# Context products of A, B and D as split products with the values stationary, with moved stages, in a hybrid five-branch decoder trunk

## What is computed

```python
pr = split_projection(x @ w_in)              # D_MODEL 1024 -> all branches' q, k, v, z, g
o_a = dsa_attention(aq, ak, av, iq, ik, pr['i_w'])   # causal, top 128 keys of an index score
o_b = moba_attention(bq, bk, bv)             # here: causal over both blocks of 256
o_c = rms_norm(diff_attention(cq, ck, cv, lam), diff_norm) * (1.0 - lam_init)
o_d = mla_attention(qn, qr, kn, kr, dv)      # causal, from low-rank latents
o_e = memory_attention(e_q, mk, mv)          # 256 memory tokens
# each: s = q k^T * scale; p = softmax(s); o = p v
y = o * jax.nn.silu(z)
u = jnp.einsum('btnc,ncd->btnd', y, w_branch)
out = jnp.sum(jax.nn.sigmoid(g) * u, axis=2) @ w_out
x = layer_norm(DN_ALPHA * x + out, ln_g, ln_b)
```

## Time and profile before

| | us |
|---|---|
| median of 3 runs | 1381.6 |
| range of the runs | 1380.46 to 1382.38 |
| profiled execution, its own time | 1384.15 |
| its span, first to last instruction | 1382.5 |

### The profile page before, as it was taken

The page is one execution under the profiler, slowest core; times in us unless marked ns, Lnnn a source line. Parts: engine busy times, 40 slices in busy tenths (PEclk is TensorE's granted clock), DMA queues, the critical chain, the costliest instruction groups (busy, mean ns, idle before and its releaser), DMA issues.

```text
span 1382.5 us, 19021 instructions
## 1 busy us (share of the span) xinstructions
PE 1328.0 (96%) x6872; PEld 1130.7 (82%) x6872; DVE 661.8 (48%) x1609; ACT 653.3 (47%) x1296; POOL 669.9 (48%) x850
## 2 busy tenths in 40 slices
PE   6999999999988999999999999999999899999995
PEld 5888878888877898888888888888888779888884
DVE  4646696433155753213265668753322665432044
ACT  4455345454275664423245543555434665643232
POOL 3543453255563444467464435334446434645764
PEclk9899999999998999999999999999999999999998
DMA  7322242231331143232413223223123213323221
GB/s 258 114 77 62 81 114 58 67 88 47 103 95 37 37 123 107 58 107 77 140 49 106 68 71 106 81 58 85 53 74 111 59 33 86 95 65 100 84 77 61
DMA packets 147052, 116.47 MB, mean 84 GB/s; under 512 B 5520, under 2 KB 131856, under 8 KB 146704
## 3 DMA queue, kind: packets, MB, share of 16 engines
q1 hardware_dynamic: 146816, 114.22, 27.8%
q10 hardware_dynamic: 144, 1.05, 0.2%
HBM read 112.10 MB, written 3.15 MB: 83 GB/s over the span
## 4 chain that ended last, share of the span: by engine, by line
PE 79%; DVE 12%; ACT 4%; issue 2%; POOL 1%; DMA 1%; SPq 0%; POOLq 0%; DVEq 0%; ACTq 0%
PE product L737 19%; PE product L738 18%; PE product L739 18%; PE context L977 5%; PE scores L949 3%; PE transposed L962 3%; PE branch_product L737 2%; PE branch_product L739 2%; PE branch_product L738 2%; DVE index_scores L1389 2%; DVE top_eight L1395 1%; DMA residual<-in_x_dram 1%; ACT score_operands L1001 1%; POOL residual L677 1%; DVE vector_scratch L1214 1%
## 5 line engine op out<-in xcount | busy, mean ns | idle before, releaser
L721 POOL TENSOR_TENSOR weights_rest<-raw_weights,weights_head 128x320 fp32r<-128x320 f32 (+3 forms) x672 | 540.1, 836 | 376.8 <-ACT weights_head L1001 376.8
L737 PE MATMUL product<-weights_head,stationary_head 128*128 128x512 f32 (+3 forms) x768 | 291.4, 379 | 7.8 <-POOL weights_rest L721 7.6
L1001 ACT ACTIVATE weights_head<-raw_weights 128x1280 fp32r<-128x1280 f32 (+4 forms) x178 | 198.3, 1115 | 200.3 <-PE product L739 153.5
L739 PE MATMUL product<-weights_head,stationary_rest 128*128 128x512 f32 (+3 forms) x768 | 285.6, 372 | 0.0
L738 PE MATMUL product<-weights_rest,stationary_head 128*128 128x512 f32 (+3 forms) x768 | 285.4, 372 | 0.0
L737 PE MATMUL product<-stationary_head,weights_head 128*128 128x512 f32 x640 | 263.5, 412 | 0.0
L738 PE MATMUL product<-stationary_rest,weights_head 128*128 128x512 f32 x640 | 252.6, 395 | 0.0
L739 PE MATMUL product<-stationary_head,weights_rest 128*128 128x512 f32 x640 | 252.1, 394 | 0.0
L704 POOL TENSOR_TENSOR merged<-merged,activated 128x256 f32<-128x256 f32 x128 | 93.0, 748 | 291.4 <-DVE activated L1533 291.2
L737 PEld LDWEIGHTS product<-weights_head,stationary_head 128*128 128x128 f32 x768 | 145.7, 190 | 29.8 <-POOL weights_rest L721 8.4
L739 PEld LDWEIGHTS product<-weights_head,stationary_rest 128*128 128x128 f32 x768 | 145.4, 189 | 23.7
(11 more groups left out here) (200 smaller groups left out, 1812.5 us busy)
## 6 DMA issues: line engine op xcount, KB each, us to landing
raw_weights<-in_w_in_dram SPq DMA_DIRECT2D x104, 512.0 KB, 3.7
raw_weights<-in_w_in_dram SPq DMA_DIRECT2D x72, 256.0 KB, 2.9
raw_weights<-in_w_branch_dram SPq DMA_DIRECT2D x80, 128.0 KB, 3.7
raw_weights<-in_w_out_dram SPq DMA_DIRECT2D x16, 512.0 KB, 3.6
merged<-in_w_mem_kv_dram SPq DMA_DIRECT2D x8, 512.0 KB, 7.3
raw_weights<-in_w_in_dram SPq DMA_DIRECT2D x8, 416.0 KB, 3.1
raw_weights<-in_w_in_dram SPq DMA_DIRECT2D x8, 296.0 KB, 3.8
residual<-in_x_dram SPq DMA_DIRECT2D x4, 512.0 KB, 11.4
```

The costliest lines, as they stand in the source:

```text
L721: ins = nc.gpsimd.tensor_tensor(WL[:, sw, part], RAW[:, sr, part], WH[:, sw, part].bitcast(F32), ALU.subtract)
L737: nc.tensor.matmul(dst, sh, mh, start=start, stop=False)
L739: return nc.tensor.matmul(dst, sl, mh, start=False, stop=stop)
L1001: return nc.scalar.activation(dst, src, ACT.Copy, scale=scale)
```

## The change

- **Contexts of A, B and D.** `wide_steps` takes the place of `att_steps` for them. The transposed probabilities of two tiles are kept side by side, ACT's copy as fp32r heads, and DVE makes their rests (`pr`, new tile of 1024 columns), after which alone TP is free. The values of a head are split as well (`vs` on ACT, `vr` on DVE): head and rest, 64 columns each, are one stationary operand of 128. A context product moves 256 (both tiles) or 128 (the diagonal block of the second) columns of heads or rests of the probabilities. There is one `V` for two tiles. Bank O then holds the context transposed, the part by the values' heads in one half of the rows and that by their rests in the other: ACT copies one (`fo`), DVE adds the other (`fa`).
- **Gates.** 1/row sum is multiplied into the gate (`fin`), the gate is transposed (`zj`, bank G2 or TP), and DVE multiplies it into the context; `yj` is then a copy and a subtraction from SBUF, without transposes.
- **Places** of B, A and C attention, top of tile 3, A out and lambda are moved.
- **C.** The operand copies and rests are cut into four parts a head; the join `W` and the transposes `T` lie further apart; its first transposes use banks U and O.
- **Order of groups** in IX and O1, of the first steps, and of the norms at a layer's end; the fourth tile of x is loaded after two weight units; `ahead` is gone.

```diff
+WIDE = "ABD"
+def wide_steps(b):
+    if b == "D":
+        out = [[("qt", b, 0)], [("ev", b, 0)], [("er", b, 0), ("qt", b, 1)], [("ev", b, 1)], [("er", b, 1)], [("vs", b, 0), ("vr", b, 0)]]
+    else:
+        out = [[("qt", b, 0)], [("ev", b, 0), ("er", b, 0)], [("ev", b, 1), ("er", b, 1)], [("vs", b, 0), ("vr", b, 0)]]
+    for i in range(UNITS + LAG_V + 1):
+        first, second = [], []
+        u = i - LAG_V
+        j = u // NT
+        if 0 <= u < UNITS and u % 2 == 1:
+            first.append(("V", b, u))
+        if 0 <= i - LAG_T < UNITS:
+            first.append(("T", b, i - LAG_T))
+            second.append(("pr", b, i - LAG_T))
+        if u >= NT and u % NT == 0:
+            first.append(("fa", b, j - 1))
+            if j < NH:
+                second.append(("vr", b, j))
+        if i < UNITS:
+            second.append(("S", b, i))
...
+        out += [first, second]
...
-    ("B attention", ("gE0", 1, 0), ("gE1", 3, 3), 0.0),
-    ("top of tile 3", ("gE0", 0, 1), ("gE1", 2, 3), 0.0),
+    ("B attention", ("gE0", 0, 1), ("gE1", 3, 3), 0.0),
+    ("top of tile 3", ("gE0", 2, 0), ("gE1", 3, 4), 0.0),
-    ("A attention", ("gB0", 0, 2), ("gB1", 3, 3), 0.0),
-    ("A out", ("gB1", 3, 4), ("C0", 0, 3), 0.0),
-    ("lambda", ("gB1", 3, 3), ("C0", 0, 2), 0.0),
-    ("C attention", ("gA0", 0, 0), ("D0", 3, 2), 0.0),
+    ("A attention", ("gB0", 0, 2), ("C0", 1, 2), 0.0),
+    ("A out", ("C0", 1, 3), ("C0", 2, 2), 0.0),
+    ("lambda", ("gB0", 2, 0), ("gB0", 2, 0), 0.0),
+    ("C attention", ("C1", 0, 2), ("D0", 3, 1), 0.0),
...
+            order = [(0, 0), (1, 0), (0, 1), (1, 1), (2, 0), (2, 1), (0, 2), (1, 2), (0, 3), (2, 2), (1, 3), (2, 3)] + [(3, t) for t in range(NT)]
+        elif c == "O1":
+            order = [(0, t) for t in range(NT)] + [(1, 0), (1, 1), (2, 0), (3, 0), (2, 1), (3, 1)] + [(u, t) for t in (2, 3) for u in range(1, 4)]
...
-    start = [("ln0", 0), ("ln0", 1), ("mkv", 0), ("ln0", 2), ("xj", 0, 0), ("xj", 0, 1), ("ln0", 3), splits[0], ("mkv", 1),
-             ("xj", 1, 0), ("xj", 1, 1), ("ln0", 4), splits[1], splits[2]]
+    start = [("ln0", 0), ("ln0", 1), ("mkv", 0), ("ln0", 2), ("xj", 0, 0), ("xj", 0, 1), splits[0], splits[1], ("ln0", 3), ("mkv", 1),
+             ("xj", 1, 0), ("xj", 1, 1), splits[2], ("ln0", 4)]
...
+                    elif kind == "V" and step[1] in WIDE:
+                        _, b, u = step
+                        j, t = divmod(u, NT)
+                        ph, pl, vs = wide(b)
+                        if t == 1:
+                            claim("O")
+                            pe.wait_ge(rest.sem, rest.at(L, ("vr", b, j)))
+                        pe.wait_ge(rest.sem, rest.at(L, ("pr", b, u)))
+                        blocks = [(0, ph), (t, ph), (t, pl)] + [(i, p) for i in range(1, t) for p in (ph, pl)]
+                        blocks.insert(3 if t == 1 else 1, (0, pl))
+                        for n, (i, p) in enumerate(blocks):
+                            at = P if i == t else 0
+                            last = nc.tensor.matmul(O[:, (t - 1) * P + at:(t + 1) * P], vs[:, i].rearrange("p c d -> p (c d)"),
+                                                    p[:, i, at:2 * P], start=n == 0, stop=n == len(blocks) - 1)
...
-                        freed["TP"] = (moved, L, step)
+                        freed["TP"] = (rest, L, ("pr", b, u)) if b in WIDE else (moved, L, step)
```

More of the change, by code:

```diff
@@ L131, in diff_steps @@
             first.append(("S", "C", 2 * i))
[L132 removed]
+            second.insert(0, ("S", "C", 2 * i + 1))
         if 0 <= i - 1 < UNITS:
[L134 to L146 removed]
+            first.append(("W", i - 1))
+        if i == 3:
+            second.append(("qt", "C", 1))
+        out += [first + early.get(2 * i, []), second + early.get(2 * i + 1, [])]
     return out
@@ L587, in _ @@
             load_mk(0, 2)
-            load_x(3)
             load_mk(0, 3)
@@ L858, in _ @@
                         freed[name] = (rest, L, ("x", t, j))
+                    elif kind == "yj" and step[1] in WIDE:
+                        continue
+                    elif kind == "zj":
+                        _, b, k = step
+                        name, bank = z_bank(k)
+                        claim(name)
+                        pe.wait_ge(final.sem, final.at(L, (b, 2 * k + 1)))
+                        for t in range(NT):
+                            last = nc.tensor.transpose(bank[:, t * P:(t + 1) * P],
+                                                       VZ[:, vz(b), t, BW + k * P:BW + (k + 1) * P], ident)
+                        last.then_inc(t_done.sem, t_done.step(step))
+                        freed[name] = (gated, L, step)
                     elif kind == "yj":
@@ L1119, in _ @@
                         act.wait_ge(t_done.sem, t_done.at(L, step))
-                        copy(PT[:, 0:w], TP[:, 0:w]).then_inc(moved.sem, moved.step(step))
+                        if b in WIDE:
+                            half = slice(t % 2 * P, (t % 2 + 1) * P)
+                            copy(wide(b)[0][:, 0:t + 1, half], TP[:, 0:w].rearrange("p (i n) -> p i n", n=P)).then_inc(moved.sem, moved.step(step))
+                        else:
+                            copy(PT[:, 0:w], TP[:, 0:w]).then_inc(moved.sem, moved.step(step))
                     elif kind == "lam":
```

233 lines of the change are left out of this document (158 added, 75 removed).

## The result

The changed kernel takes 1367.4 us (median of 4 runs, 1366.2 to 1369.6) against 1381.8 before (median of 4 runs; the 1381.6 above is that of three of them): a ratio of 0.9899, 95% interval 0.9882 to 0.9916. The forecast was 1350. The direction was right, and of 32 us of gain 14.4 came. The profiled execution has a span of 1368.0 against 1382.5.

What follows compares the result with a forecast made beforehand. TensorE was taken as the bound, busy 1328.0 of 1382.5 us. The terms -17 + 10 + 4 - 3 + 6 - 21 - 4.5 - 1.5 - 5 sum to -32, from the median 1381.6 to 1350 us; range 1330 to 1374.

Steps and rivals of the forecast that it cites:

- Contexts, -17: Context products of A, B and D: 1.40 us a head, 0.70 less, over 24 heads; -17 us.
- rival 4: Units of A, B and D: chained transposes, copy and rest outgrow their cover; at 0.5 us a unit +48, 1398; chance 0.05.
- B's new wait, +10: Start of gE0: B's earlier first transposes wait 4.9 us a layer for B0's last rotation on DVE; +10 us.
- The clock behind it, +4: Behind B's new wait the clock falls to half and stays low 4 to 5 us; +4 us in both layers.
- B's old wait and DVE's lag, -3 + 6: B attention: second scores' 1.5 us wait a layer goes, -3; DVE, 93% busy, lags 3 us a layer, +6.
- Rival 1: B's stage: DVE becomes the bound and lags 10 us a layer; 1364 us, chance 0.18.
- C, -21: C attention: waits for joined maps and operand rests go through new step order and longer stretch; -21 us.
- Start, -4.5: Kernel start: first groups run at 28.8, second weight wait won, later order costs about a microsecond; -4.5 us.
- Boundary, -1.5: Layer boundary: the 2.26 us wait for second weights goes, early split removed at no cost; -1.5 us.
- Tail, -5: After the last product: tile-by-tile order ends the span at +12.3, not +17.1; -5 us.
- exclusive lock: B's stage: SBUF-only DVE subtractions lock against GpSimd's reads; about 2 us a layer, sum 4 more, not included.

Runs made afterwards that it cites:

- experiment 3: Changed kernel with A's four rotations of queries and keys moved from under B0 to under B1; 1362.4 us.
- experiment 5: Changed kernel with 20 unread products of 512 columns added ahead of the wait for the last rotation, before B's first transposes; 1363.9 us.
- experiment 9: Kernel of experiment 2 with 14 of the 16 rounds of tile 3's selection left out; 1352.3 us.
- experiment 11: Changed kernel with C's attention back at its old place and first banks, its new order of steps kept; 1365.3 us.
- experiment 6: Changed kernel with the old order of IX's and O1's groups, start and layer norm steps, the early split still out; 1375.8 us.
- experiment 2: Changed kernel with only the places of B's attention and of the top of tile 3 put back as before; 1358.0 us.
- experiment 4: Changed kernel with 20 unread products of 512 columns added behind the wait for the last rotation, ahead of B's first transposes; 1379.2 us.

## Why the prediction was right or wrong

By the table, the 17.6 us that did not come are about 5.6 in B, 4.6 in D, 2.8 at the boundary, 2.3 in C, 1.6 in A and 1.3 at the start, less 0.5 that the tail gave on top.

**Contexts, -17: wrong step.** The price of the products was right (1.39 to 1.49 us a head for 1.40; from start to next start they save 2.2 us a branch and layer, 13 in all, for a base that was 2.04 and not 2.1). What failed is "in A and D DVE is otherwise light and I cost both at nothing: the cover is the products between two units". I compared the work of a unit with the time of a unit. What counts is the latency of the chain from transposes through ACT's copy and DVE's rest to the context, with whatever ACT and DVE have in order ahead of it. One case in D, all engines:

```profile
578.48 1.28 ACT L1097 ACTIVATE weights_head<-raw_weights 128x1280 fp32r<-128x1280 f32 x1 [0.77 <-PE branch_product L803]
...
579.66 0.58 ACT L1097 ACTIVATE key_rests<-transposed 128x512 fp32r<-128x512 f32 x1
...
580.27 0.69 DVE L1444 TENSOR_TENSOR probabilities_T_rest<-transposed,key_rests 128x512 fp32r<-128x512 f32 x1 [1.09 <-ACT key_rests L1097]
```

A weight copy that has nothing to do with attention stands ahead of the copy, and DVE, idle for 1.09 us, makes the rest too late: 0.97 us of TensorE. In D such waits (from start to start; the first is one of transposes) are 0.32, 0.53 and 0.97 = 1.8 a layer, which leaves 0.4 of 2.2, and the stages say 0.5. In A they are 0.75 and 0.35, which leaves 1.1; measured 1.36. In B they are larger than the gain. Each of the narrow contexts needed ACT's copy alone. This mechanism was on record as rival 4, the handshake of a unit, with a chance of 0.05 and a price of 48 us; it ate about 13, or 0.14 us for each of the 96 units.

**B's new wait, +10: right** (9.5, in the place and of the size forecast). It was not "DVE saturated" alone: experiment 3 puts 1.9 of the 4.7 us to that, and the rest to a place two groups behind the product that it needs. **The clock behind it, +4: right** (3.2 by the stages, 3.5 by the medians, experiment 5). But the sum had no second fall, and there is one, behind the context that waits 1.7 us in B: 3.4 us at half level, so 1.7 a layer in this execution.

**B's old wait and DVE's lag, -3 + 6: right in kind, too small.** The old wait went. In layer 0 the contexts wait 1.86 and 0.69 and lose 1.7 to the clock, 4.2 where I had a lag of 3 a layer. The reason was wrong too. I had DVE at 51 of 55 us, 93%, over the 30 groups; there the changed kernel shows 48.7 of 62.3, 78%:

```profile
207.90:270.20 62.30, 60.02 (x310) 49.62 (x309) 48.69 (x116) 32.24 (x67) 20.43 (x24) 0.97 0.22 60
```

The work was nearly as counted, and TensorE's waits made the stretch longer. Rival 1, DVE as the bound, gave 1364, nearest to the result, and it holds for about half of the waits at most (experiment 9, the rounds left out). That its number is near is luck.

**C, -21: nearly right in size (-18.7 by the stages), wrong in cause, so the size is partly luck.** The term rested on new order and new stretch together. The order, with the cut copies, gives 11.7 and 11.0 us in the two layers (experiment 11), and the earlier start takes back 2.4 and 1.6. The first transposes did not wait for C0's last rotation; what came late was a maximum behind DVE's gates, 2.1 us in one piece.

**Start, -4.5: right** (-3.2 in the profiled execution, -4.2 to -5.0 in ten kernels with the same start). The waits moved to the next rests, as forecast, but the index transposes a few groups on then stood one group too near to their staging on DVE, 1.0 us. **Boundary, -1.5: +1.3.** The step that failed is that the early split "is removed at no cost under the same cover": it was worth 1.5. And E's 1.15 was not seen at all: an order of groups moved the products of IX nearer to their first reader. **Tail, -5: right** (-5.5, all of it the order, experiment 6).

The page's rule that I weighed, of an exclusive lock between GpSimd and a DVE instruction with both inputs in SBUF (the Trainium skill, "SBUF — State Buffer", section "Who interferes with whom"), stood outside the sum. The changed kernel's timeline agrees with it at the very wait:

```profile
187.39 3.37 POOL L785 TENSOR_TENSOR weights_rest<-raw_weights,weights_head 128x320 fp32r<-128x320 f32 x4 [2.43 <-ACT weights_head L1097]
...
188.27 0.89 DVE L1331 TENSOR_TENSOR vector_scratch<-staged_features,consts_sb 128x64 f32<-128x64 f32 x1
...
191.16 0.22 DVE L1331 TENSOR_TENSOR vector_scratch<-staged_features,consts_sb 128x64 f32<-128x64 f32 x1
```

The same step takes 0.89 us beside GpSimd and 0.22 without it. In experiment 3 the last rotation's four steps take 3.3 us where a whole rotation without GpSimd takes 0.9 (0.22 + 0.22 + 0.28 + 0.29, less overlaps): by these rows GpSimd's rests are 2.4 of the 2.83 us that were left. No kernel with them moved away was run, so that share is argued.

**What stays open:** whether another order of ACT's steps (weight copy behind the transposed probabilities) would free the wide form's 2.2 us a branch. The two orders tried for B gained nothing or lost. Open too are the exact share of DVE's load in B, and what decides whether the clock falls behind a wait of 1 to 3 us.

## What to carry over

When a faster form of a product puts one more engine between its operand and its start, count the latency of the whole chain with everything that ACT and DVE have in order ahead of each step, not the work of a unit against its time: here 13 us of TensorE's own work were saved and 13 paid back in waits and in the half clock behind them. A consumer placed nearer to its producer, or a producer moved nearer to its consumer by an order of groups, needs the same sum. And of a change in many parts, undo each alone: two of these (B's places, B's wide form) cost 15 us together and hid what the rest gained.

## What the hardware showed that I had not expected

A short wait can cost its length twice, and a wait of the same length need not. In the changed kernel a wait of 1.69 us at 233.42 is followed by 3.4 us at half clock (234.90 to 238.30, above). In the kernel of experiment 2 a wait of 1.74 us at 223.27 is not: TensorE's row, and two stretches behind it.

```profile
223.27 0.70 PE L1056 MATMUL context<-score_operands 128*128 128x256 f32 x4 [1.74 <-DVE score_operands L1436]
```
```profile
224.50:226.50 2.00, 2.00 (x12) 1.66 (x11) 1.74 (x6) 0.77 (x4) 1.07 (x2) 1.00 0.03 8
226.00:229.00 3.00, 3.00 (x18) 2.49 (x16) 1.90 (x5) 2.68 (x6) 0.00 (x0) 1.00 0.75 213
```

These are two different waits. But the wait of 1.69 us itself does the same. Six kernels have the same instructions there (the changed one and those of experiments 3, 4, 5, 6 and 11), and in their twelve layers the clock fell behind it six times. In experiment 3 it fell in layer 0 and not in layer 1:

```profile
229.70 1.39 PE L1056 MATMUL context<-score_operands 128*128 128x256 f32 x8 [1.69 <-DVE score_operands L1444]
897.33 1.20 PE L1056 MATMUL context<-score_operands 128*128 128x256 f32 x8 [1.69 <-DVE score_operands L1444]
```
```profile
230.60:233.90 3.30, 3.30 (x11) 2.72 (x10) 2.44 (x7) 0.30 (x2) 0.00 (x0) 0.50 0.63 182
897.40:900.80 3.40, 3.40 (x20) 3.06 (x21) 3.19 (x11) 0.88 (x3) 0.00 (x0) 1.00 0.69 193
```

So it is not the program's order that tells them apart. C's wait of 2.1 us shows it too: in the twelve kernels with C's new place the clock fell behind 9 of 24. All ten waits of 4.7 us, and both of 2.8 in experiment 3, came with a fall, but 3.4 us at half clock followed some of them and 6.8 others. The price of a wait of 1.7 us is therefore between once and twice itself. And one stage can differ by 0.9 us (gA0) to 1.4 us (gE1) between two layers or two kernels that run the same instructions in it; a smaller difference of these stages in one profile shows nothing.
